# A gather ring laid under the second block's tensors, with the output weights fetched into it, a reordered scan start and key transposes behind the first projection

## The reference, cut to what matters

```python
h_ctx = ctx * (1 + csc1) + csh1
... = _project(h_ctx, ...)               # q, k (after a depthwise conv), v, o, gates, attention q/k/v
hm_c, st_f, st_b = _mlstm_bidir(qm_c, km_c, vm_c, gt_c, zero, zero)
h_lat = x * (1 + sc1) + sh1
... = _project(h_lat, ...)
hm, _, _ = _mlstm_bidir(qm, km, vm, gt, st_f, st_b)   # scan in chunks of 128, both directions
qa, ka = _rope_2d(rms_norm(qa)), _rope_2d(rms_norm(ka))
att = _attn_latent(qa, ka, va, ka_c, va_c)            # 8 heads, 2 key/value heads, 512 x 768 scores
mix = concat([_mlstm_out(hm, om, w), att]) @ w_out
x = layer_norm(ALPHA * x + g1 * mix)
y = _peer(x * (1 + sc2) + sh2, wq, keys, u, v)        # 8 heads, top 16 of 128 x 128 experts per token
x = layer_norm(ALPHA * x + g2 * y)
```

## Time and profile before

| | us |
|---|---|
| median of 3 runs | 4027.12 |
| the profiled execution | 4033.01 |
| its span | 4031.2 |
| `second_project`, from the first context multiply | 2104 to 2357 |
| `second_heads`, up to the first attention transpose | 2357 to 2456 |
| `second_heads`, attention | 2456 to 2596 |
| `route_peer`, up to the first gather | 2596 to 2664 |
| `route_peer`, gathers and the end | 2664 to 4031 |

### The profile page before, as it was taken

One profiled execution on the slowest core, in us unless ns is written; L12 is line 12 of the kernel. 1 busy time (PEld: TensorE's weight loads), 2 busy tenths in 40 slices (PEclk: granted clock), 3 DMA queues, 4 the chain that ended last, 5 costly groups with the idle time before them and its releaser, 6 DMA issues. The chain is left out here.

```text
span 4031.2 us, 37513 instructions
## 1 busy us (share of the span) xinstructions
PE 3406.1 (84%) x11902; PEld 1511.2 (37%) x11903; DVE 1940.7 (48%) x3995; ACT 677.4 (17%) x1600; POOL 941.4 (23%) x811
## 2 busy tenths in 40 slices
PE   7988999668899987999868967789878888788877
PEld 3345444422233322333225445444333333333332
DVE  5834222522233322333225236476666766677676
ACT  1011211000000000000002125312222222222221
POOL 2000000022122222021221040014444444444443
PEclk8999999789999999999989988789999899899998
DMA  9825423369998998296975100239999999999997
GB/s 332 281 105 177 168 101 133 125 242 408 371 384 346 365 407 347 96 389 262 383 305 183 53 7 1 84 125 408 421 421 409 421 410 412 421 405 421 416 421 317
DMA packets 194149, 1157.36 MB, mean 287 GB/s; under 512 B 25659, under 2 KB 27995, under 8 KB 74356
## 3 DMA queue, kind: packets, MB, share of 16 engines
q1 hardware_dynamic: 97140, 565.17, 36.2%
q0 software_dynamic: 80576, 564.05, 34.1%
q10 hardware_dynamic: 16320, 26.75, 2.1%
HBM read 1128.96 MB, written 48.68 MB: 292 GB/s over the span
## 5 line engine op out<-in xcount | busy, mean ns | idle before, releaser
L1149 PE MATMUL ps<-wt,e_xT 128*64 128x512 f32 x3200 | 741.1, 608 | 115.5 <-DMA wt<-in_w_exp 114.7
L2559 DVE SCALAR_TENSOR_TENSOR mod<-q_uv,mix 128x1024 f32<-128x1024 f32 x512 | 627.1, 1225 | 389.7 <-DMA q_uv<-in_peer_uv,q_picks 384.4
L2264 POOL DMA_INDIRECT q_uv<-in_peer_uv,q_picks x512 | 573.5, 1120 | 997.4 <-PE ps L2356 715.8
L2356 PE MATMUL ps<-q_uv,q_dg 128*128 128x512 f32 x1024 | 517.3, 662 | 136.8 <-ACT q_dg L2433 136.7
L2356 PE MATMUL ps<-q_uv,tri 128*128 128x512 f32 x1024 | 474.7, 618 | 80.8 <-ACT tri L2433 80.4
L1129 POOL COPY wt<-e_land 128x2048 f32<-128x2048 f32 x124 | 247.9, 2029 | 1002.7 <-PE ps L1149 951.1
L1149 PEld LDWEIGHTS ps<-wt,e_xT 128*64 128x64 f32 x3200 | 219.5, 139 | 595.5 <-issue 381.6
L2356 PEld LDWEIGHTS ps<-q_uv,q_dg 128*128 128x128 f32 x1024 | 212.2, 212 | 432.9 <-issue 432.9
L1149 PE MATMUL ps<-wt,e_aT 128*64 128x512 f32 x1600 | 354.8, 596 | 2.8 <-ACT e_aT L1202 2.8
L2356 PEld LDWEIGHTS ps<-q_uv,tri 128*128 128x128 f32 x1024 | 198.5, 198 | 353.4 <-issue 353.4
L454 PE MATMUL ps<-hT,wt 128*128 128x512 f32 x640 | 285.1, 602 | 1.5 <-DVE wt L781 1.5
(11 more groups left out here) (447 smaller groups left out, 3411.8 us busy)
## 6 DMA issues: line engine op xcount, KB each, us to landing
wt<-in_w_exp SPq DMA_DIRECT2D x260, 1024.0 KB, 19.3
e_land<-in_w_exp SPq DMA_DIRECT2D x124, 1024.0 KB, 24.1
wt<-in_w_in_units SPq DMA_DIRECT2D x15, 2048.0 KB, 11.3
mod<-in_w_mod_units SPq DMA_DIRECT2D x48, 512.0 KB, 5.6
scratch_xs<-const_zeros SPq DMA_DIRECT2D x8, 2080.0 KB
mod<-in_w_ada_units SPq DMA_DIRECT2D x32, 512.0 KB, 8.5
p_ring<-in_w_in SPq DMA_DIRECT2D x7, 2048.0 KB, 10.4
e_xg<-scratch_xs ACTq DMA_DIRECT2D x104, 128.0 KB, 6.9
```

What stands on the lines that cost most here:

```text
L1149: ins = nc.tensor.matmul(ps[64 * h:64 * h + 64, at, :], lhs[:, k % 4, 64 * (k // 4):64 * (k // 4) + 64], wt[:, u, a, h * W:(h + 1) * W], s ...
L2264: pool.indirect_dma_start(out=uv[:, n % NR, :, :].rearrange("p a d -> p (a d)"), out_offset=None, in_=A["peer_uv"], in_offset=bass.Indirec ...
L2356: last = nc.tensor.matmul(acc(t)[:, c, :], dg(n), uv[:, n % NR, 1, c * W:(c + 1) * W], start=fresh, stop=closing)
L2559: dve.scalar_tensor_tensor(junk[:, n % 2, :], uv[:, n % NR, 0, :], 1.0, mix[:, tile_of(k), :], ALU.mult, ALU.mult, accum_out=ap[:, k % 2, ...
```

## The change

`uv`, the gather ring, is allocated before the second block's tensors, and `ct`, `va`, `ko` and `zr` become views into it. The context part of `hT` moves into `mix`'s spare room (`hTc`), where the context's modulation row lay; ScalarE's first copy into it waits until that row has been read. The gate bias `bg` is fetched at the end of `second_project` instead of at the start of `second_heads`. The squares move from GpSimd to ScalarE (behind Ln), and their sum on VectorE moves from before the cumulative sums to behind `aa`. `spreads(3)` goes ahead of `states(0)`, and `spreads(4)` and `spreads(5)` ahead of `states(1)`. SP fetches both units of `w_out` in `second_heads`, once the scan's last matmuls are done (`s_nm`), into the ring's first four slots. In `route_peer` gather n goes to slot (n + 4) mod 10, so gathers 6 to 9 fall on `w_out` and gather 5 on the keys, as before. TensorE runs `project(0)` once two tiles are transposed, then the key transposes, then `project(1)`.

```diff
@@ build
+        uv = sb("uv", [P, NRING, 2, D])
...
+            flat = uv[:, :, :, :].rearrange("p n a d -> p (n a d)")
+            TA, NA = T + TC, NT + NTC
...
+            S = dict(ct=parts[0], va=parts[1].rearrange("p (t h c) -> p t h c", t=NA, h=MH), ko=parts[2],
+                     zr=parts[3].rearrange("p (t c) -> p t c", t=NA), bg=sb("bg", [P, 16], c=second), flat=flat)
...
@@ second_project
-        hT = sb("hT", [P, KD, TA])
+        hT = sb("hT", [P, KD, T])
+        hTc = modc.rearrange("p (k t) -> p k t", k=KD)
...
+                sp.dma_start(S["bg"][:, :], A["b_gates_2"].unsqueeze(0).broadcast_to([P, 16])).then_inc(s_bg, 16)
                 sp.wait_ge(s_g2, 16)
+                sp.wait_ge(s_bg, 16)
...
-                    t = NT + i if i < NTC else i - NTC
+                    dst, t = (hTc, i) if i < NTC else (hT, i - NTC)
+                    if i == 0:
+                        act.wait_ge(s_h, NTC)
...
@@ second_heads, SP
-                sp.dma_start(bg[:, :], A["b_gates_2"].unsqueeze(0).broadcast_to([P, 16])).then_inc(s_bg, 16)
...
+                sp.wait_ge(s_nm, 2 * NT)
+                for u in range(2):
+                    sp.dma_start(S["flat"][:, u * KD * W:(u + 1) * KD * W], A["w_out_2_units"][u]).then_inc(s_wout[u], 16)
@@ second_heads, GpSimd
-                pool.tensor_tensor(sq[:, :, :], zr[:, :, 16:16 + 10 * DH], zr[:, :, 16:16 + 10 * DH], ALU.mult).then_inc(s_sq, 1)
@@ second_heads, TensorE
-                spreads(0)
-                spreads(1)
-                spreads(2)
+                for i in range(4):
+                    spreads(i)
                 states(0)
-                spreads(3)
+                spreads(4)
+                spreads(5)
                 pe.wait_ge(s_C, 1)
                 states(1)
-                spreads(4)
-                spreads(5)
@@ second_heads, ScalarE
+                act.activation(sq[:, :, :], zr[:, :, 16:16 + 10 * DH], ACT.Square).then_inc(s_sq, 1)
@@ second_heads, VectorE
-                dve.wait_ge(s_bg, 16)
...
-                dve.wait_ge(s_sq, 1)
-                link(dve.tensor_reduce(rq[:, :, :].rearrange("p t h -> p (t h)"),
-                                       sq[:, :, :].rearrange("p t (h c) -> p (t h) c", c=DH), AX_X, ALU.add))
-                dve.tensor_scalar(rq[:, :, :], rq[:, :, :], 1.0 / DH, RMS_EPS, ALU.mult, ALU.add).then_inc(s_rq, 1)
...
                 dve.wait_ge(s_aa, 1)
+                dve.wait_ge(s_sq, 1)
+                link(dve.tensor_reduce(rq[:, :, :].rearrange("p t h -> p (t h)"),
+                                       sq[:, :, :].rearrange("p t (h c) -> p (t h) c", c=DH), AX_X, ALU.add))
+                dve.tensor_scalar(rq[:, :, :], rq[:, :, :], 1.0 / DH, RMS_EPS, ALU.mult, ALU.add).then_inc(s_rq, 1)
@@ route_peer
+    SHIFT = NR - WOUT
...
+        keys = uv[:, (KEYS + SHIFT) % NR].rearrange("p a d -> p (a d)").rearrange("p (c d) -> p c d", c=2 * PH)
+        wout = uv[:, 0:SHIFT].rearrange("p n a d -> p (n a d)").rearrange("p (u k w) -> p u k w", u=2, k=KD)
...
+            return (n + SHIFT) % NR
...
-                for u in range(2):
-                    sp.dma_start(wout[:, u].rearrange("p k w -> p (k w)"), A["w_out_2_units"][u]).then_inc(s_wout[u], 16)
-                    if u == 0:
-                        sp.dma_start(keys, A["peer_keys_2"].rearrange("h a k d -> k (h a) d")).then_inc(s_keys, 16)
+                sp.dma_start(keys, A["peer_keys_2"].rearrange("h a k d -> k (h a) d")).then_inc(s_keys, 16)
...
+                pe.wait_ge(s_tT, 2)
+                project(0)
                 pe.wait_ge(s_keys, 16)
...
                 pe.wait_ge(s_tT, NT)
+                project(1)
                 pe.wait_ge(s_kT, 1)
-                project(0)
-                project(1)
                 first_queries(0)
```

More of the change, by code:

```diff
@@ L44 @@
 PAIRS = PH * PK
+NRING = 10
 TAKEN = []
@@ L94, in build @@
         mix = sb("mix", [P, NT, D])
+        uv = sb("uv", [P, NRING, 2, D])
         with ExitStack() as second:
[L96 to L99, removed]
+            flat = uv[:, :, :, :].rearrange("p n a d -> p (n a d)")
+            TA, NA = T + TC, NT + NTC
+            ends = [0]
+            for n in (8 * TA, NA * MH * (MD + 1), (NA + NT) * MH * MD, NA * 784):
+                ends.append(ends[-1] + n)
+            parts = [flat[:, a:b] for a, b in zip(ends, ends[1:])]
+            S = dict(ct=parts[0], va=parts[1].rearrange("p (t h c) -> p t h c", t=NA, h=MH), ko=parts[2],
+                     zr=parts[3].rearrange("p (t c) -> p t c", t=NA), bg=sb("bg", [P, 16], c=second), flat=flat)
             kept = (NT + NTC) * MH * MD
@@ L104, in build @@
             end_stage(nc)
-            second_heads(nc, A, K, dram, ident, tri, mod, ps, S, mix)
+            s_wout = [nc.alloc_semaphore(f"q_wout{u}") for u in range(2)]
+            second_heads(nc, A, K, dram, ident, tri, mod, ps, S, mix, s_wout)
             end_stage(nc)
-        route_peer(nc, A, K, dram, ident, tri, mod, x, ps, mix, out)
+        route_peer(nc, A, K, dram, ident, tri, mod, x, ps, mix, out, uv, s_wout)
 def first_mix(nc, A, K, dram, ident, tri, mod, x, ps, yT, hT, qkv, ring, mT, gB):
@@ L1596, in _, with second_heads @@
                             last.then_inc(s_conv, 1)
-def second_heads(nc, A, K, dram, ident, tri, mod, ps, S, mix):
+def second_heads(nc, A, K, dram, ident, tri, mod, ps, S, mix, s_wout):
     AHEADS, AKV, REP = 8, 2, 4
@@ L1656, in second_heads @@
         rd = sb("rd", [P, 2, AKV])
-        s_bg, s_load, s_dve, s_abs, s_lf1, s_one, s_lf2, s_lf = (sem(n) for n in ("bg", "load", "dve", "abs", "lf1", "one", "lf2", "lf"))
+        s_load, s_dve, s_abs, s_lf1, s_one, s_lf2, s_lf = (sem(n) for n in ("load", "dve", "abs", "lf1", "one", "lf2", "lf"))
         s_cum, s_aa, s_ab, s_ar, s_ek, s_xk, s_eq, s_xq, s_wsc = (sem(n) for n in (
@@ L2032, in _ @@
                 dve.tensor_scalar(eq[:, 1], eq[:, 1], -1.0, None, ALU.mult).then_inc(s_eq, 1)
+                dve.wait_ge(s_xk, 1)
+                state(1)
                 dve.wait_ge(s_xq, 1)
@@ L2140, with route_peer @@
 ORDER = (0, 2, 1, 3)
-def route_peer(nc, A, K, dram, ident, tri, mod, x, ps, mix, out):
+def route_peer(nc, A, K, dram, ident, tri, mod, x, ps, mix, out, uv, s_wout):
     BATCH = PK
     NBATCH = NT * PH
-    NR, ND, G = 10, 8, 4
+    NR, ND, G = NRING, 8, 4
     TOTAL = NBATCH * BATCH
@@ L2198, in route_peer @@
         s_keys, s_ln1, s_ln2, s_tm, s_tT, s_kt, s_kT = (sem(n) for n in ("keys", "ln1", "ln2", "tm", "tT", "kt", "kT"))
-        s_wout = [sem(f"wout{u}") for u in range(2)]
         s_wq = [sem(f"wq{u}") for u in range(2)]
@@ L2205, in route_peer, with slot @@
         s_iot, s_link, s_g, s_ex, s_gr, s_r = (sem(n) for n in ("iota", "link", "g", "ex", "gr", "r"))
+        def slot(n):
+            return (n + SHIFT) % NR
         def dg(n):
@@ L2355, in _ @@
                     for c in range(2):
-                        last = nc.tensor.matmul(acc(t)[:, c, :], dg(n), uv[:, n % NR, 1, c * W:(c + 1) * W],
+                        last = nc.tensor.matmul(acc(t)[:, c, :], dg(n), uv[:, slot(n), 1, c * W:(c + 1) * W],
                                                 start=fresh, stop=closing)
```

21 lines of the change are left out of this document (9 added, 12 removed).

## The result

The changed kernel takes 3990.36 us (median of 4 runs, 3983.99 to 3995.55) against 4027.09 us of the kernel before (median of 4 runs); the ratio is 0.9914, 95% interval [0.9894, 0.9933]. Forecast were 3992.0 us and a range of 3984 to 4006. Its profiled execution took 3994.46 us with a span of 3992.7, 38.5 us shorter than the one before.

A forecast was written before the change was run, and what follows sets the result against it. The prediction took the DMA-limited gather stream as the bound, shifted by what precedes it. Gains of 8.8 + 10.6 + 15.7 = 35.1 us turn 4027.1 into 3992.0 us; own range 3986 to 3998, whole range 3984 to 4006.

The forecast's parts named there:

- What bounds it, and one for one: Steady gathers run at their own DMA rate, 417 GB/s; the end moves as much as the first gathers move.
- Term 1: Start of `second_heads`, gates and sums: without waits for bias, GpSimd's squares and their sum, the stage gains 8.8 us.
- Term 2: Recurrence in `second_heads`: with the spreads reordered, VectorE's waits ahead of steps 3 and 4 (3.80, 6.81 us) vanish; 10.6 us.
- Term 3: Output projection in `route_peer`: `project(0)` starts 14.7 us earlier, gains 3.0 from the high clock, loses 2.0 to keys; 15.7 us.
- What costs nothing: `w_out`'s 4 MB during the attention, ScalarE's new wait and the bias fetch in `second_project` were claimed to cost nothing.
- The attention, 0 with ends of 6: Attention loop of TensorE, VectorE and ScalarE: another clock phase can move it either way; put at 0, ends 6 us.
- The low clock: Rival: TensorE's clock stays low where taken high; gain 26.4 us, time 4000.7 us; chance 0.12.
- GpSimd in VectorE's way: Rival, first chunks of the scan: GpSimd and VectorE hinder each other; 5 us, time 3997 us; chance 0.06.
- The 0.26 us of the earlier trace: An 8-element VectorE update under GpSimd's later work, read as showing little contention when GpSimd's instructions are short.
- Term 3 reached the end whole: Rival denied here: something unmoved sets the gather stream's start, so the output projection's gain is lost; 4007.7 us; chance 0.06.
- The gathers kept 414 to 416 GB/s: Rival denied here: turned slots slow the gather stream, 12.9 us per per cent, 4037 us at 3.5%; chance 0.04.
- The sum: Whole kernel: 8.8 + 10.6 + 15.7 = 35.1 us gained, median 3992.0 us.

The follow-up runs named there:

- the repeat: The changed kernel run again without any edit, for its spread: 3994.38 us (3990.28 to 3995.66), ratio 0.9911 to the kernel before.

## Why the prediction was right

- **What bounds it, and one for one.** Held. The page alone did not show it, though: the earlier trace rows gives TensorE the same 15% as the DMA, and it is the stretches of the earlier trace rows that name the gathers. From the first dot product to the end 1332.5 and 1332.9 us, 1329.6 to 1335.8 in all profiles, whatever came ahead.
- **Term 1, 8.8 us.** Measured 8.8 (15.26 to 6.45 us). The steps held: the table load set Exp's start (2356.86, as it ended), Square took 3.39 us where 3.5 were taken, and the first reduction started behind the sum 4.33 us after `aa`, where the spreads alone had set 4.36. That GpSimd and not the bias was the larger wait was read from one row (4.11 us for 96 elements, ending with the squares), and the experiments confirm it: 5.9 us for GpSimd, 2.7 for the sum, 2.2 for the bias once the rest is gone.
- **Term 2, 10.6 us.** The mechanism held, the size was low: 13.0 in the first profile, about 12.4 over the eight profiles with the new order (mean 70.9 against 83.3). Three things are off. The second state's move was overlooked; it takes 2.1 us out of the chain of maxima, but VectorE does it later, and at most 1.8 us are left. In the kernel as it was forecast (state put back) the maxima took 21.0 us where 30.2 - 10.6 = 19.6 were forecast: one update was held 1.0 us by GpSimd, and VectorE once waited 0.76 us for TensorE. And the scan proper was taken to keep its length, but from the last reduction's start to the attention's first transpose it took 48.7 us before and 46.2 with the state put back, which more than made up for it. The two traces show where: TensorE runs the same matmuls faster. The first chunk's states and products took 2.54 and 3.15 us before (granted clock 0.68) and 2.05 and 1.95 with the state put back (1.00), and the last products, before and in the changed kernel:

```profile
2450.77 3.35 PE L1801 MATMUL ps<-va,h_sT 128*128 128x129 f32 x16 [2.30 <-ACT h_sT L1907]
```

```profile
2428.68 2.05 PE L1814 MATMUL ps<-uv,h_sT 128*128 128x129 f32 x16 [2.29 <-ACT h_sT L1921]
```

The wait ahead of them is the same; the granted clock was 0.58 and 1.00. So what the forecast missed goes with TensorE's clock in code that no edit touched. All three profiles with the old order are slow at both places; of the nine with the new spreads two are slow at the first and three at the second (3.19 to 3.66 us). Whether the order brings the clock along or chance does stays open.
- **Term 3, 15.7 us.** Measured 16.0. `project(0)` started 1.8 us into the stage and not 2.0, the rest as forecast. The 3.0 us for the low clock were one profile's: against the kernel with all terms undone, whose slow records took 5.37 us and not 6.57, the same stretch is 14.7 us shorter (45.8 to 31.1).
- **What costs nothing.** Held: with the terms undone the ratio is 0.9997. The fetch of `w_out` during the attention is not seen in its length either: 139.1 to 143.0 us in the nine profiles that have it there, 140.4, 141.9 and 144.2 in the three that don't.
- **The attention, 0 with ends of 6.** 2.4 us longer in the profile, within the 139.1 to 144.2 us that unchanged code shows.
- **The rivals.** The low clock did not come back where it was priced. GpSimd in VectorE's way is real (1.20 us for 8 elements). Where each VectorE instruction of the scan is set against the shortest of its kind, the excess adds up to 0.9 us in two traces with the old order and to 2.8 to 3.6 us in three with the new one, so I estimate 2 to 3 us for this rival, which had 5. It lies in a stretch that still came out shorter than forecast. The 0.26 us of the earlier trace rows were no sign that short GpSimd instructions cost little: that update started 0.24 us before GpSimd's 1.27 us ended, the held one 0.09 us behind a start. Term 3 reached the end whole. The gathers kept 414 to 416 GB/s.
- **The sum.** 35.1 us forecast; 37.8 measured in the three terms, 38.5 in the span, 36.7 in the medians, and 34.9 in the medians of the repeat. That the first median lies within 1.6 us of the forecast is partly luck: the repeat's, 3994.38 us, is 4.0 us above the first.

## What to carry to other kernels

When a short instruction takes microseconds and ends with another engine's, move the other engine's work before hurrying its inputs: here the early bias alone gained 0.2 of 8.8 us. An in-order engine that serves a critical recurrence and something that waits should do the recurrence's work first. Waits that run beside each other hide each other's price, as GpSimd's hold hid the late bias; where taking away one leaves another, as with fetch and order (5.7 and 8.0 us alone, 16.0 together), only the last removal also keeps TensorE's clock up.

## What the runs showed that I had not expected

- GpSimd holds a `tensor_scalar` of VectorE with one input as well as additions with two: 6.52 us for a pair in one profile, 6.53 in another, where it took 0.26 without GpSimd.
- An instruction that gets ahead of GpSimd by 0.08 us is not held at all (0.26 us); the next one is.
- Nearly the same code before `second_heads` ends up to 8.8 us apart from one profile to another, as much as the whole of term 1. In a kernel of 4000 us such an edit is seen in a stage's own length, not in the time.
